# Modulation chunks of the second layer at two norms, and the first layer's modulation loaded and turned by feature halves

## What is computed

```
sh_a, sc_a, g_a, sh_f, sc_f, g_f = split(silu(c) @ mod_w[l] + mod_b[l], 6)   # the modulation, 6 x 1024 values
h = rms_norm(x, norm_mix_g[l]) * (1 + sc_a) + sh_a
x = x + g_a * (mixer(h) @ w_out[l])
h = rms_norm(x, norm_ffn_g[l]) * (1 + sc_f) + sh_f
x = x + g_f * swiglu(h, ffn_w_in[l], ffn_w_out[l])
```

## Time and profile before

| what | us |
|---|---|
| median of 3 runs | 2386.36 (2381.99 to 2386.81) |
| profiled execution, first to last instruction | 2379.8 |
| PE busy | 2292.7 (96%) |
| DVE busy | 1496.3 (63%) |
| ACT busy | 1028.4 (43%) |
| PE at layer 0's front: first tile product | 37.5 |
| PE at layer 0's feed-forward norm: w_out's last product ends, feed-forward starts | 317.4, 331.9 |
| PE at layer 1's mixer norm: last ffn_out product ends, od_q starts | 721.1, 735.3 |

### The profile page before, as it was taken

The page is one execution under the profiler, slowest core; times in us unless marked ns, Lnnn a source line. Parts: engine busy times, 40 slices in busy tenths (PEclk is TensorE's granted clock), DMA queues, the critical chain, the costliest instruction groups (busy, mean ns, idle before and its releaser), DMA issues.

```text
span 2379.8 us, 32080 instructions
## 1 busy us (share of the span) xinstructions
PE 2292.7 (96%) x13686; PEld 1954.9 (82%) x13686; DVE 1496.3 (63%) x1893; ACT 1028.4 (43%) x1256; POOL 0.2 (0%) x4
## 2 busy tenths in 40 slices
PE   6998989999998999999999999999999999999997
PEld 3775667777786878888998878999989987789997
DVE  4777543333346576765877767666678767767475
ACT  4255441121225265544663435444555534435343
POOL 0000000000000000000000000000000000000000
PEclk9999989999998999999999999999999999999999
DMA  8530034444422252555555544454555545345552
GB/s 329 206 148 1 36 126 193 159 195 159 159 106 107 88 125 89 195 188 205 215 185 178 184 171 160 178 191 178 179 188 196 187 176 198 141 178 183 177 183 101
DMA packets 61397, 389.12 MB, mean 164 GB/s; under 512 B 6600, under 2 KB 11080, under 8 KB 16072
## 3 DMA queue, kind: packets, MB, share of 16 engines
q1 hardware_dynamic: 61256, 387.08, 44.7%
HBM read 386.01 MB, written 1.05 MB: 163 GB/s over the span
## 4 chain that ended last, share of the span: by engine, by line
PE 86%; DVE 7%; ACT 4%; issue 2%; DMA 1%; SPq 0%; DVEq 0%; ACTq 0%
PE PS L509 23%; PE PS L511 23%; PE PS L510 23%; PE PS L615 5%; PE PS L613 3%; PE PS L864 1%; DMA raw<-chunks_in 1%; PE PS L1041 1%; DVE w_lo L1722 1%; ACT w_hi L1244 1%; ACT xn L1322 1%; PE PS L743 1%; PE PS L1023 1%; PE PS L703 1%; PE PS L768 1%
## 5 line engine op out<-in xcount | busy, mean ns | idle before, releaser
L1722 DVE TENSOR_TENSOR w_lo<-raw,w_hi 128x2048 fp32r<-128x2048 f32 x300 | 683.4, 2290 | 492.7 <-ACT w_hi L1244 491.6
L1244 ACT ACTIVATE w_hi<-raw 128x2048 fp32r<-128x2048 f32 x300 | 571.6, 1912 | 696.8 <-PE PS L511 323.8
L509 PE MATMUL PS<-x_hi_lo,w_hi 128*128 128x256 f32 (+1 forms) x1760 | 546.2, 310 | 9.7 <-DVE x_hi_lo L1787 5.2
L511 PE MATMUL PS<-x_hi_lo,w_lo 128*128 128x256 f32 (+1 forms) x1760 | 543.4, 309 | 0.0
L510 PE MATMUL PS<-x_hi_lo,w_hi 128*128 128x256 f32 (+1 forms) x1696 | 518.6, 306 | 0.0
L509 PEld LDWEIGHTS PS<-x_hi_lo,w_hi 128*128 128x128 f32 x1760 | 337.1, 192 | 36.3 <-issue 19.6
L511 PEld LDWEIGHTS PS<-x_hi_lo,w_lo 128*128 128x128 f32 x1760 | 337.0, 191 | 16.8
L510 PEld LDWEIGHTS PS<-x_hi_lo,w_hi 128*128 128x128 f32 x1696 | 325.1, 192 | 14.0
L509 PE MATMUL PS<-w_hi,x_hi_lo 128*128 128x512 f32 (+1 forms) x800 | 317.9, 397 | 15.6 <-DVE x_hi_lo L1787 10.8
L510 PE MATMUL PS<-w_lo,x_hi_lo 128*128 128x512 f32 (+1 forms) x800 | 313.5, 392 | 0.0
L511 PE MATMUL PS<-w_hi,x_hi_lo 128*128 128x512 f32 (+1 forms) x800 | 313.5, 392 | 0.0
(11 more groups left out here) (326 smaller groups left out, 2666.1 us busy)
## 6 DMA issues: line engine op xcount, KB each, us to landing
raw<-chunks_in SPq DMA_DIRECT2D x348, 1024.0 KB, 4.8
bias_ring<-brows_in SPq DMA_DIRECT2D x32, 256.0 KB, 5.0
G<-nrows_in SPq DMA_DIRECT2D x2, 1536.0 KB, 6.7
BIG<-rel_in SPq DMA_DIRECT2D x4, 512.0 KB, 7.7
free_b<-rel_in SPq DMA_DIRECT2D x4, 512.0 KB, 7.8
tabt<-tabs_in SPq DMA_DIRECT2D x1, 1536.0 KB, 11.7
X<-x_in SPq DMA_DIRECT2D x1, 1024.0 KB, 8.5
X<-ctx_in SPq DMA_DIRECT2D x1, 1024.0 KB, 10.5
```

The costliest lines, as they stand in the source:

```text
L509: pe.matmul(o, lhs[0], rhs[0], start=start, stop=False, **more)
L511: return pe.matmul(o, lhs[1], rhs[0], start=False, stop=stop, **more)
L1244: act.activation(w_hi[:, i % HI_RING, :], ring[:, n % RING, :], ACT.Copy).then_inc(*hi_ready.now(n))
L1722: dve.tensor_tensor(w_lo[:, c % RING, :], ring[:, c % RING, :], w_hi[:, i % HI_RING, :].bitcast(F32), ALU.subtract).then_inc(*lo_ready.now(c))
```

## The change

- **Front.** Layer 0's first 8 modulation chunks become two packs: (0, 2), for the lower features, and (1, 3), for the upper. The first pack's four chunks stay ahead of all; then comes ev_in's first chunk, then the second pack's four, then ev_in's second chunk. X and the context are loaded after the first chunk instead of after the second. Nine early chunks (0 to 8) have a place of their own (six in BIG, three in ring slots), so SP waits for none of them. PE runs the second pack inside ev_in's first chunk, after its second feature tile, and turns it after the third. ACT interrupts the norm after tile 3: it copies the pack, waits for the upper modulation, splits ev_in's second chunk, and goes on with tiles 4 to 7.
- **Feed-forward norm of layer 0.** Four chunks of layer 1 (j = 0, 1) stand in the list between w_out's last pair and f0. PE runs two before `root_of_squares`, one inside it (`beside`, between the sums and the spreading) and one after it.
- **Feed-forward of layer 0.** 16 modulation chunks instead of 24.
- **Mixer norm of layer 1.** The last four chunks (j = 10, 11) stand between ffn_out's last chunk and o0. PE runs three before the sums and one beside. Their copy is ACT's `modulation(7)`, after the norm and before `split_for("od_q", 1, 1)`.
- A finished pack is turned after the next pack's first two chunks instead of before them. There is one pack more (8 instead of 7).

The diff, cut to its core:

```diff
-MOD_PARTS = (((0, 1, 2, 3), (4, 5, 6, 7, 10, 11), (8, 9)), (tuple(range(12)),))
-MOD_PACKS = [(0, (0, 1, 2, 3)), (0, (4, 5, 6, 7)), (0, (10, 11)), (0, (8, 9)),
+MOD_PARTS = (((0, 2), (1, 3), (4, 5, 6, 7, 10, 11), (8, 9)), ((0, 1, 2, 3, 4, 5, 6, 7), (8, 9, 10, 11)))
+MOD_PACKS = [(0, (0, 2)), (0, (1, 3)), (0, (4, 5, 6, 7)), (0, (10, 11)), (0, (8, 9)),
              (1, (0, 1, 2, 3)), (1, (4, 5, 6, 7)), (1, (8, 9, 10, 11))]
-MOD_BANKS = 2
+MOD_BANKS = (5, 6, 6, 5, 6, 5, 6, 5)
+EARLY = 9
+EARLY_SLOTS = {4: 0, 7: 1, 8: 2}
...
+        def slot_of(c):
+            return (3, 1, 2, 0)[(c - EARLY) % RING] if c >= EARLY else EARLY_SLOTS[c]
+        def held_before(c):
+            return c - RING if c >= EARLY + RING else {EARLY + 1: 7, EARLY + 2: 8, EARLY + 3: 4}.get(c)
+        def raw_of(c):
+            if c < EARLY and c not in EARLY_SLOTS:
+                at = CHUNK * (c - (c > 4))
+                return big(at, CHUNK)
+            return ring[:, slot_of(c), :]
...
                             for kt in range(KC):
                                 pe.wait_ge(*copied_v.after(tiles_of, kt))
                                 for b in range(2 * groups):
                                     mm = product(PS[:, b, 0:width], lhs(kt, b), [a[:, kt, 0:width] for a in w], kt == 0, False)
+                                if at_tile and kt in at_tile:
+                                    at_tile[kt]()
...
                 mm.then_inc(*sums_bc.now(key))
+                if beside:
+                    beside()
                 pe.wait_ge(*rstd_diag.after(key))
...
                 if first:
-                    mod_turn()
                     claim(b)
...
                 used(c)
+                if i == 0 and kg == 1:
+                    mod_turn()
+                if i == last and kg == 1:
+                    state["unturned"] = n
...
+                def second_rows():
+                    mod_pair()
+                    mod_pair()
-                ev_in(0, mods(1, 2), ("mix", 0))
+                ev_in(0, mods(0, 2), ("mix", 0), {1: second_rows, 2: lambda: mod_end(0, 1)})
...
-                between = None if l else mod_row
+                between = None if l else mod_pairs(8)
...
-            for _ in range(4):
-                mod_chunk()
+            mod_pair()
             root_of_squares(("mix", 0), 4, 0)
-            for _ in range(4):
-                mod_chunk()
+            mod_pair()
             mod_end(0, 0)
             even_mixer()
             project_feat("w_out", 0, 2, y4T, width=512, freed=updated("w_out", 0), need=copied("y0"), between=mod_row)
-            mod_end(0, 2)
-            root_of_squares(("ffn", 0), 4)
+            mod_pair()
+            mod_end(0, 3)
+            root_of_squares(("ffn", 0), 4, beside=mod_chunk)
+            mod_chunk()
             swiglu(0, 4)
-            root_of_squares(("mix", 1), 4)
-            project_tok("od_q", 1, 2, KD, tokens(hT[4]), 1, tiles_of=("mix", 1))
+            mod_pair()
+            mod_chunk()
+            root_of_squares(("mix", 1), 4, beside=mod_chunk)
+            project_tok("od_q", 1, 2, KD, tokens(hT[4]), 1, tiles_of=("mix", 1),
+                        between=at_steps({1: lambda: mod_end(1, 1)}))
...
-                if c == 2:
+                if c == 1:
                     sp.dma_start(X[:, 0, :, :], x_d).then_inc(*x_in.now(by=16))
                     sp.dma_start(X[:, 1, :, :], ctx_d).then_inc(*x_in.now(by=16))
-                if c >= RING:
-                    sp.wait_ge(*projected.after("used", c - RING))
+                if held_before(c) is not None:
+                    sp.wait_ge(*projected.after("used", held_before(c)))
...
-            norm_mod(("mix", 0), 4, 0, lambda: split_to(first_ev + 1))
+            def second_half():
+                modulation(1)
+                act.wait_ge(*mods_ready.after(0, 1))
+                split_to(first_ev + 1)
+            norm_mod(("mix", 0), 4, 0, second_half, 3)
...
-            modulation(3)
+            modulation(4)
             root_mod(("ffn", 0), 4)
-            norm_mod(("ffn", 0), 4, 2, lambda: split_to(first + 5))
+            norm_mod(("ffn", 0), 4, 3, lambda: split_to(first + 5))
...
             norm_mod(("mix", 1), 4, 0)
+            modulation(7)
             split_for("od_q", 1, 1)
...
-            norm_mod(("mix", 0), 4, KD, (0, 0), None, lambda: lo_to(ev))
+            norm_mod(("mix", 0), 4, KD, (0, 0), lambda k: modulation(0, 1) if k == 3 else None, lambda: lo_to(ev))
...
-            mod_next(8)
+            mod_next(4)
...
-                mod_next((1, 2, 2, 2, 1, 2)[n])
+                mod_next((4, 2, 2, 2, 2, 2)[n])
...
         among(weight_chunks(i["w_out"][l]), 2)
+        if l == 0:
+            mod_next(4)
         n0 = 0
         for n in FF_PARTS[l]:
-            among(weight_chunks(paired(i["ffn_w_in"][l])[:, 512 * n0:512 * (n0 + n)]), 2)
-            among(weight_chunks(i["ffn_w_out"][l][256 * n0:256 * (n0 + n)]), 2)
+            in_w = weight_chunks(paired(i["ffn_w_in"][l])[:, 512 * n0:512 * (n0 + n)])
+            out_w = weight_chunks(i["ffn_w_out"][l][256 * n0:256 * (n0 + n)])
+            for weights in (in_w, out_w):
+                for i_w, w in enumerate(weights):
+                    chunks.append(w[None])
+                    if i_w % 2 and len(mods) > 4:
+                        mod_next(2)
             n0 += n
+        mod_next(4)
```

More of the change, by code:

```diff
@@ L363, in build_program @@
         w_in = [ev(f"w_in{i}") for i in range(RING)]
+        early_in = {c: ev(f"early_in{c}") for c in range(EARLY) if c not in EARLY_SLOTS}
         bias_in = [ev(f"bias_in{i}") for i in range(2)]
@@ L401, in build_program, with arrival @@
         hidden = ev("hidden")
+        def slot_of(c):
[7 more added lines that the diff above has]
+            return ring[:, slot_of(c), :]
+        def arrival(c):
+            return early_in[c] if c < EARLY and c not in EARLY_SLOTS else w_in[slot_of(c)]
         def gate(l, kind, k, who):
@@ L645, in sum_of_squares, with root_of_squares @@
                 reader[b] = std_ready.after(key)
-            def root_of_squares(key, tiles, bank=7):
+            def root_of_squares(key, tiles, bank=7, beside=None):
                 acc, n = sums[tiles][0], tiles * P
@@ L883, in mod_row, with mod_pairs, between @@
                     mod_chunk()
+            def mod_pairs(n):
+                left = [n]
+                def between(kg):
+                    if kg == 1 and left[0]:
+                        left[0] -= 1
+                        mod_row(kg)
+                return between
             def lora(st, first, k_tiles, width):
@@ L1240, in split_to @@
                     state["split"] += 1
-                    act.wait_ge(*w_in[n % RING].after(n))
+                    act.wait_ge(*arrival(n).after(n))
                     if i >= HI_RING:
                         act.wait_ge(*projected.after("used", chunks[i - HI_RING]))
-                    act.activation(w_hi[:, i % HI_RING, :], ring[:, n % RING, :], ACT.Copy).then_inc(*hi_ready.now(n))
+                    act.activation(w_hi[:, i % HI_RING, :], raw_of(n), ACT.Copy).then_inc(*hi_ready.now(n))
             def split_up_to(c):
@@ L1307, in root_mod, with norm_mod @@
                                scale=1.0 / D).then_inc(*std_ready.now(key))
-            def norm_mod(key, tiles, part, middle=None):
+            def norm_mod(key, tiles, part, middle=None, at=4):
                 l, kind = key[1], 0 if key[0] == "mix" else 3
@@ L1324, in norm_mod @@
                     ins.then_inc(*full_ready.now(key, k))
-                    if k:
+                    if k and not (at == 3 and k == 4):
                         high(k - 1)
-                    if k == 4 and middle:
+                    if k == at and middle:
+                        if at == 3:
+                            high(k)
                         middle()
@@ L1406, in modulation @@
                     act.wait_ge(*mod_turned.after(n - 4))
-                act.activation(mod_rows_of(n), PS[:, 5 + n % MOD_BANKS, :], ACT.Copy).then_inc(*mod_rows.now(n))
+                act.activation(mod_rows_of(n), PS[:, MOD_BANKS[n], :], ACT.Copy).then_inc(*mod_rows.now(n))
             def swiglu(l, tiles):
@@ L1478, in _ @@
             root(("daq", 1), 16, 64)
-            modulation(1)
+            modulation(2)
             split_to(first_ev + 6)
@@ L1502, in _ @@
             split_to(first_ev + 8)
-            modulation(2)
+            modulation(3)
             copy_turned("daq")
@@ L1567, in _ @@
             root_mod(("ffn", 1), 2)
-            act.wait_ge(*mods_ready.after(1, 0))
+            act.wait_ge(*mods_ready.after(1, 1))
             for k in range(KD):
@@ L1981, in modulation @@
                 js = sorted(MOD_PARTS[l][part])
-                dve.wait_ge(*mod_turned.after(max(n for n, (layer, _) in enumerate(MOD_PACKS)
-                                                  if layer == l and n <= (0, 2, 3)[part] + 6 * l)))
```

(2 more changed lines are left out.)

55 lines of the change are left out of this document (29 added, 26 removed).

## The result

The changed kernel takes 2417.94 us (median of 4 runs, 2414.55 to 2419.09) against 2384.65 for the one before (2381.99 to 2386.81): a ratio of 1.0136, 95% interval 1.0122 to 1.0151. It is 33 us slower; 2415.7 was forecast. The profiled execution is 2417.3 us long. Against the 2379.8 of before that is 37.5, more than the medians differ, because the profiled execution of before was its quickest (2381.99 us) and that of the changed kernel its slowest (2419.09 us).

A forecast was written before the change was run, and what follows sets the result against it. PE, busy for 96% of the span, was taken as the bound, its stops as what the change touches. Front 9.3, feed-forward norm 14.5 and mixer norm 5.5 sum to 29.3 us; 2386.4 + 29.3 = 2415.7 us, range 2400 to 2424.

The forecast's parts named there:

- Front: Start of layer 0: first tile 5.9 us earlier, but ev_in's second chunk 6.4 later; in sum +9.3 us.
- Feed-forward norm: Layer 0: f0 lands 17.7 us later and holds the norm; +17.7 and +0.6, less 3.8 for four chunks, +14.5.
- The restart: PE at ev_in's second chunk: after a 9.4 us stop it restarts at the low clock, losing 1.9 us.
- f0's place in the list: Feed-forward's first chunk, behind four moved ones: its slot frees later, three loads precede it, it lands at 329.1 us.
- The price of a chunk: Modulation chunks moved out of the dense feed-forward: 0.96 us each at full clock, 7.7 for eight, 3.84 at each norm.
- Mixer norm of layer 1: o0's split falls behind the norm, so od_q's second chunk starts 9.3 us later; less 3.8 for four chunks, +5.5.
- Only f0's wait costs: Rival: front and layer 1's norm come out even, only the feed-forward norm loses; 2401 us, chance 0.13.
- The gaps are filled: Rival: moved chunks hold no look-ahead split, f0 lands in time, PE works through the gaps; about 2371 us, chance 0.06.

The follow-up runs named there:

- e1: Kernel before the change with only the new front; list and order at both norms stay old: 2397.75 us, ratio 1.0056.
- e5: Changed kernel with two modulation chunks instead of four ahead of f0, the other two back in the feed-forward, none beside the norm: 2413.84 us.
- e3: Changed kernel with f0's split moved behind the feed-forward norm's squares on ACT and DVE: 2401.64 us, ratio 1.0070.
- e8: Kernel before, list and loads untouched; PE runs a modulation pair in its idle time before the feed-forward tiles, f1's split moves ahead of them: 2379.42 us.
- e9: Kernel before plus eight chunks at the two norms, f0's split behind the squares and o0's split mid-norm: 2385.52 us, ratio 1.0005.
- e11: Kernel before with only the modulation pair moved into PE's idle time before the feed-forward; f1's split stays: 2383.28 us, ratio 0.9988.
- e10: Kernel before with only f1's split moved ahead of the feed-forward tiles, no pair in PE's idle time: 2385.26 us, ratio 1.0002.

## Why the prediction was right

It held in sign and size (29.3 us forecast, 33.3 measured), and each of the three stops is there. The forecast time looks closer than that (2415.7 and 2417.9), because it started from 2386.4 and the kernel before came out at 2384.65 in the result. Its steps:

- **Front.** The first tile came at 33.2, not 31.6: the sums and the spreading took 1.87 and 2.08 us instead of 1.05 and 1.17 before, the lengths that they have at the low clock, so that the scaling began at 23.77 and not at 22.15. The chunks behind it took 3.46 us for two, as forecast. The stop before the second chunk was forecast at 9.4 us and is 9.27; with the late first tile that chunk starts 7.9 us later than before, not 6.4. The restart was undersized: 5.4 us at the low clock, 2.6 us lost and not 1.9 (in e1 and e5 the same restart ran low for 3.1 us only). With the one chunk more that is still to come (1.0) this makes 11.5. Forecast +9.3, measured +11.9 at w_out's end and +12.3 in e1.
- **Feed-forward norm.** That f0's place in the list sets the norm was right (e3, e5). Two terms were undersized. f0 was to land 11.7 us after w_out's end and landed 13.6 after it. The forecast took the end of the data flow, 326.5 us, for the landing of the third load; in that trace it was issued at 319.4 and landed 8.5 us later, at 327.9. And the turn of the pack, which I left at its old length, ran at the low clock (1.84 us instead of 1.06). Forecast +18.3, measured +21.0.
- **The price of a chunk.** Forecast 0.96 us from the chunk's own busy time. The feed-forward got 9.4 us shorter. In the trace of before a pair looks like this:

```profile
355.36 0.39 PE L511 MATMUL PS<-x_hi_lo,w_lo 128*128 128x512 f32 x1
355.67 1.92 PE L864 MATMUL PS<-raw,bias_ring 128*32 128x512 f32 x16
357.53 0.50 PE L509 MATMUL PS<-x_hi_lo,w_hi 128*128 128x512 f32 x1
357.87 0.40 PE L510 MATMUL PS<-x_hi_lo,w_hi 128*128 128x512 f32 x1
```

Products there start every 0.23 us. From the product before the pair to the second one behind it are 2.51 us, so the pair costs 2.05, which is 1.03 for a chunk and 8.2 for eight. Another 0.9 is a turn: before, three stood in the feed-forward (at 451, 547 and 644 us), now two (at 438 and 535), and the third at 783 us in od_q, behind the last mark. So of the 1.7 us more than forecast about half is not saved, only moved.
- **Mixer norm of layer 1.** Forecast +9.3 until od_q's second chunk, measured +9.3 (33.2 against 23.9). That it fits to the tenth is luck: od_q started 25.7 us after ffn_out's end, forecast 25.0, and its 24 products took 7.4 us, forecast 8.1.
- **The rivals.** "Only f0's wait costs" is out: each of the other two stops was taken away alone and gave 7.9 and 6.2 us. "The gaps are filled" is out for this list; e8 shows the same idea working where neither a load nor a split is pushed back.

## What to carry to other kernels

When a piece of work is moved in a list that several engines follow, ask first which look-aheads count places in that list and which loads wait for its slots: here three splits stood behind waits, and placing them better gave back 16.3, 6.2 and at most 7.9 us, where the moved work is about 4 us at each place. To fill an engine's idle time, reorder only that engine and take data whose loads are under way and are not delayed by it. A second obstacle hides behind the first: removing f0's split (e9) uncovered a load 5 us long, and by the trace the raised clock (e11) paid only together with f1's earlier split (e8).

## What was not expected of the hardware

- PE's raw modulation chunks, products with only 32 columns of weights, raise the granted clock as dense products do: behind two of them it stood at 0.93 to 1.00 (e8), while in the same place without them it was 0.50 (e10). In the changed kernel it had risen as well before the feed-forward, behind the chunk that follows the spreading, and was back at 0.50 when the tile products came, after a stop of 3.56 us:

```profile
361.00:363.00 2.00, 0.26 (x4) 0.00 (x0) 0.91 (x3) 1.64 (x4) 0.00 (x0) 0.92 0.60 176
365.00:367.00 2.00, 2.00 (x5) 1.61 (x6) 1.57 (x4) 2.00 (x5) 0.00 (x0) 0.50 0.16 66
```

  In e8 and e11, where it stayed up, the stop before the first tile was 1.43 and 1.57 us. No run changes the stop alone.
- A load's landing comes later than its data. In the changed kernel five loads were issued between 329.4 and 335.5 us and landed 4.9, 7.5, 9.1, 10.7 (f0) and 9.8 us after their issue: at 334.3, 337.9, 340.4, 342.9 and 345.3, one every 2.5 us behind the second. Nearly all their data had come by 344, 1.3 us before the last landing (stretches, last two columns DMA share and GB/s):

```profile
342.00:344.00 2.00, 0.00 (x0) 0.00 (x0) 0.00 (x0) 1.10 (x1) 0.00 (x0) 0.50 0.83 352
344.00:346.00 2.00, 0.00 (x0) 0.00 (x0) 1.16 (x1) 1.32 (x2) 0.00 (x0) 0.50 0.04 16
```

  Before, it was the same: the flow of the three loads ended at 326.5, and the last of them landed at 327.9.
